# Two linked model blocks on one core: the up projections of the MLPs as 64-row matmuls in pairs

## The chip, the cores and the metric

One core of a Trainium2 chip runs the whole program in one launch. The metric is device microseconds (us) of that core. The kernel before was run twice: 2519.97 and 2526.85 us, median 2523.41 us.

## The reference

Two blocks of a language model work one after the other on one sequence of 512 tokens with width 1024, in float32. The first holds a gated convolution branch, a recurrent branch and an MLP; the second holds an HGRN mixer with an MLP and an attention layer with low-rank keys and values with another MLP. Only the MLPs bear on this case. There are three, all of the same form:

```
h = rms_norm(x, g)                              # 512 x 1024
f = square(relu(h @ w_up))                      # 512 x 4096
x = x + f @ w_down                              # 512 x 1024
```

## The kernel before

All activations lie feature-major: a tile is 128 features (partitions) x 512 tokens, X has KD = 8 of them, and a matmul contracts over the 128 partitions of a weight tile and an activation tile and writes 128 x 512 sums into one of eight PSUM banks (`ps`). So that float32 accuracy comes out of matmuls on fp32r operands, every operand is split in two: a high part (XH, FH, w_hi), which is the value rounded to fp32r, and a low part (XL, FL, w_lo), which is what the rounding lost. A product is three matmuls, high x high, high weight x low activation, low weight x high activation (`product`, L1479 to L1486).

Weights come in chunks of 128 x 2048 values (1 MB), which hold two output tiles x eight contraction steps. There are two slots, 0 and 1, for raw, w_hi and w_lo, and chunk c uses slot c % 2. For each chunk SyncE loads `raw` (`load8`), ScalarE writes w_hi (`split_hi`, L549 to L553: it waits until TensorE has finished chunk c - 2, by the count of `halves`), GpSimd writes w_lo (`split_lo`, L529 to L533) and TensorE waits for that (`chunk_in`, L1500). TensorE counts up `halves` once per output tile, twice per chunk.

Each MLP (`mlp_pe`, L1605) has four quarters of the hidden width. A quarter is four up chunks (`up`, two per pass, j = 0 and 1, slots 0 and 1) and four down chunks (`down`). Up chunk j writes its two tiles to banks 2j and 2j + 1. In steady state `half8` computes the first tile entirely, 24 matmuls, and then the second (L1504). The first chunk of an MLP goes through `pair` (L1507) instead: step k of both tiles, then step k + 1, each waiting for tile k of XL, because its input is still being made; the matmul for the squares' sum of the norm (`squares_pe`) follows it. The down chunks do the same with FH and FL as input (`pair` for j = 0, `half8` for j = 1).

Behind TensorE, VectorE takes each up tile in turn (`mlp_dve`, L1146): it waits for `halves`, scales and clamps the bank into `tmp` (L1157), squares (L1160) and subtracts the high part that ScalarE writes (L707) to get FL (L1163). ScalarE, behind its second tile of a chunk, splits the weights of the chunk two further on (`mlp_act`, L700):

```
for j in range(4):
    act.wait_ge(*at(n, "t", 8 * q + 4 * i + j + 5))
    act.activation(FH[...], tmp[:, j % 2:j % 2 + 1], ACT.Square)...
    if j % 2:
        split_hi(8 * q + 2 * i + c + j // 2 + 2, j // 2)
```

So the order of the work around the change is set by each engine's own program, written out by hand, and by counted semaphores between them. Just before each MLP, a residual sum brings the tiles of X one after the other; ScalarE makes XH (L336) and VectorE makes XL of it (L352), tile by tile.

Of the kernel before, what the change touches and what calls it, by code (L numbers as in the profile page):

```python
# [11 lines left out]
KD = D // P  # L12
# [54 lines left out]
def build_program(nc, a, out):  # L67
    ctx = ExitStack()
    with ctx:
        top = [nc.sbuf_base + (-nc.sbuf_base) % 32]  # L70

        def place(name, shape, dt, at=None):

            size = int(np.prod(shape[1:])) * (1 if dt == U8 else 4)
            where = top[0] if at is None else at
            if at is None:
                top[0] += size + (-size) % 32
            return nc.alloc_sbuf_tensor_at(name, list(shape), dt, offset=where), where

        def sem(name):  # L80
            return ctx.enter_context(nc.semaphore(name))
# [3 lines left out]
        w_hi, _ = place("w_hi", [P, 2, 2048], F32R)  # L85
        w_lo, _ = place("w_lo", [P, 2, 2048], F32R)
# [85 lines left out]
        ps = ctx.enter_context(nc.psum_tensor("ps", [P, 8, T], F32))  # L172
# [5 lines left out]
        halves = sem("halves")  # L178
# [10 lines left out]
        def s_(name):  # L189

            if name not in S_:
                S_[name] = sem(name)
            return S_[name]
# [25 lines left out]
        def signals(n, what):  # L219

            if kind_of[n] == "norm":
                if what in ("hi", "lo"):
                    return 0 if n == "n_fin1" else KD
                return 1 if what in ("ln", "inv") else KD
            if kind_of[n] == "scaled":
                if what in ("hi", "lo"):
                    return KD
                return 0 if n in ("n_hg", "n_mla") else {"sq": KD, "add": KD - 1, "mean": 1, "ln": 1, "inv": 1}[what]
            if kind_of[n] == "small":
                return 1 if what in ("mean", "ln", "inv") else 2  # L230
            return {"mlp": {"t": 4 + 32, "sq": 32, "fh": 32, "fl": 4 + 32, "dn": 4 + 32}, "sum": {"x": 4 + KD}}[kind_of[n]][what]

        def sig(n, what):

            return s_(kind_of[n] + "_" + what)

        def at(n, what, value):

            stages = kinds[kind_of[n]]
            return sig(n, what), value + sum(signals(m, what) for m in stages[:stages.index(n)])  # L240
# [11 lines left out]
        def w8(t, s, n):  # L252

            v = t[:, s].rearrange("p (k n) -> p k n", k=8)
            return [v[:, k, n * P:(n + 1) * P] for k in range(8)]
# [109 lines left out]
        def squares_pe(pe, n):  # L365

            pe.wait_ge(*at(n, "add", KD - 1))
            pe.matmul(ps[:, 7], ones[:], rst[:, 0], start=True, stop=True).then_inc(sig(n, "mean"), 1)
# [1099 lines left out]
        def _(pe):  # L1468
            pe.sem_inc(halves, 4)
            pe.wait_ge(ident_in, 16)  # L1470
            for k in range(KD):
# [3 lines left out]
                for b in range(TB):  # L1475
                    mm = pe.transpose(ps[:, k % 4, b * P:(b + 1) * P], x_tm[:, b, k * P:(k + 1) * P], ident[:])
                mm.then_inc(s_("x_turned"), 1)

            def product(dst, his, los, xh, xl, start=True, stop=True):  # L1479

                n = len(his)
                for k in range(n):
                    pe.matmul(dst, his[k], xh[k], start=start and k == 0, stop=False)  # L1483
                    pe.matmul(dst, his[k], xl[k], start=False, stop=False)  # L1484
                    mm = pe.matmul(dst, los[k], xh[k], start=False, stop=stop and k == n - 1)  # L1485
                return mm  # L1486
# [10 lines left out]
            def tiles(t, n=KD, first=0):  # L1497
                return [t[:, first + k] for k in range(n)]

            def chunk_in(c):  # L1500

                pe.wait_ge(lo_done, c + 3)

            def half8(s, n, bank, xh, xl):  # L1504
                product(ps[:, bank], w8(w_hi, s, n), w8(w_lo, s, n), tiles(xh), tiles(xl)).then_inc(halves, 1)

            def pair(s, bank, xh, xl, ready=None):  # L1507

                h = [w8(w_hi, s, n) for n in range(2)]
                l = [w8(w_lo, s, n) for n in range(2)]  # L1510
                for k in range(KD):
                    if ready is not None:
                        pe.wait_ge(*ready(k))
                    for n in range(2):
                        dst = ps[:, bank + n]
                        pe.matmul(dst, h[n][k], xh[:, k], start=k == 0, stop=False)  # L1516
                        pe.matmul(dst, h[n][k], xl[:, k], start=False, stop=False)  # L1517
                        mm = pe.matmul(dst, l[n][k], xh[:, k], start=False, stop=k == KD - 1)  # L1518
                        if k == KD - 1:
                            mm.then_inc(halves, 1)  # L1520
# [4 lines left out]
            def plain(c, iters, ev, xh, xl, ready=None):  # L1525

                with pe.Fori(0, iters) as i:
                    for j in range(2):
                        chunk_in(2 * i + c + j)
                        pe.wait_ge(*ev(4 * i + 2 * j + 2))  # L1530
                        if j == 0 and ready is not None:
                            pair(0, 0, xh, xl, ready)
                        else:
                            half8(j, 0, 2 * j, xh, xl)
                            half8(j, 1, 2 * j + 1, xh, xl)
# [11 lines left out]
            for k in range(KD):  # L1547
                mm = pe.matmul(ps[:, 7], ones[:], CO[:, k], start=k == 0, stop=k == KD - 1)
# [53 lines left out]
            single(FIRST["bo"], RT, lambda v: (s_("yb_evac"), v), VGH, VGL, BO_BANKS, lambda k: (s_("vg_lo"), k + 1))  # L1602
            plain(FIRST["wo"], 2, lambda v: at("wo", "x", v), MH, ML, lambda k: (s_("ml_done"), k + 1))

            def mlp_pe(n, xh, xl):  # L1605

                c = FIRST[n]

                def up(q, i, first=False):
                    for j in range(2):  # L1610
                        chunk_in(8 * q + 2 * i + c + j)
                        pe.wait_ge(*at(n, "dn", 8 * q + 2 * j + 2))
                        pe.wait_ge(*at(n, "t", 8 * q + 4 * i + 2 * j + 2))
                        if first and j == 0:
                            pair(0, 0, xh, xl, lambda k: at("n_" + n, "lo", k + 1))
                            squares_pe(pe, "n_" + n)
                        else:
                            half8(j, 0, 2 * j, xh, xl)
                            half8(j, 1, 2 * j + 1, xh, xl)

                def down(q):
                    with pe.Fori(0, 2) as i:
                        for j in range(2):
                            chunk_in(8 * q + 2 * i + c + 4 + j)
                            if j:
                                pe.wait_ge(*at(n, "t", 8 * q + 12))
                            pe.wait_ge(*at(n, "dn", 8 * q + 4 * i + 2 * j + 2))
                            if j == 0:
                                pe.wait_ge(*at(n, "t", 8 * q + 10))

                                pair(0, 0, FH, FL, lambda k: at(n, "fl", 8 * q + 5 + k))
                            else:
                                half8(1, 0, 2, FH, FL)
                                half8(1, 1, 3, FH, FL)

                up(0, 0, first=True)
                up(0, 1)
                down(0)
                with pe.Fori(1, 4) as q:
                    with pe.Fori(0, 2) as i:  # L1640
                        up(q, i)
                    down(q)
# [124 lines left out]
            with pe.Fori(0, 4) as i:  # L1767
                def part(t, s, at, k, step, n):
                    return [t[:, s, at + q * step:at + q * step + n] for q in range(k)]
# [4 lines left out]
                for h in range(4):  # L1774
                    mm = product(ps[:, h], part(w_hi, 0, h * P, 2, 512, P), part(w_lo, 0, h * P, 2, 512, P),
                                 tiles(CQH, 2), tiles(CQL, 2))
                mm.then_inc(halves, 1)
                for h in range(2):
                    mm = product(ps[:, 4 + h], part(w_hi, 0, 1024 + h * P, 2, 256, P),
                                 part(w_lo, 0, 1024 + h * P, 2, 256, P), tiles(CQH, 2), tiles(CQL, 2))  # L1780
# [3 lines left out]
                for h in range(4):  # L1784
                    if h == 0:
                        pe.wait_ge(*at("ckv", "lo", 2))
                    pe.wait_ge(*att("qn_done", 4 * i + h + 1))
                    mm = product(ps[:, h], part(w_hi, 1, h * P, 2, 512, P), part(w_lo, 1, h * P, 2, 512, P),
                                 tiles(CKH, 2), tiles(CKL, 2))
# [7 lines left out]
                for b in range(TB):  # L1797
                    if b == 2:
                        pe.wait_ge(*att("qr_done", 2 * i + 2))
                    mm = product_x(ps[:, 4 + b], part(w_hi, 1, 1024, 2, 512, 512), part(w_lo, 1, 1024, 2, 512, 512),  # L1800
                                   [CKH[:, k, b * P:(b + 1) * P] for k in range(2)],
                                   [CKL[:, k, b * P:(b + 1) * P] for k in range(2)])
# [57 lines left out]
            for b in range(TB):  # L1860
                mm = pe.matmul(ps[:, 7, b:b + 1], rst[:, 0, b * P:(b + 1) * P], ones[:, 0:1], start=True, stop=True)
# [74 lines left out]
```

## Time and profile before

| | |
|---|---|
| median of two runs | 2523.41 us (2519.97 to 2526.85) |
| the profiled execution, its own time | 2520.08 us |
| its span, first to last instruction | 2518.3 us |
| mean granted TensorE clock | 0.967 |
| TensorE busy | 2343.5 us, 93% of the span, 10216 matmuls |
| TensorE's weight loads | 1847.8 us, beside the matmuls |
| VectorE, ScalarE, GpSimd busy | 1256.6, 910.9 and 864.5 us |

Two records stand for each matmul: its weight load (PEld) and the matmul (PE). A matmul's row runs from where it starts to where its results are written, and the next one starts before that end, so the number that counts for throughput is the distance between two starts, the pitch. In a group's name `128*128` stands for the rows and columns of weights and `128x512` for the moving operand; `64*128` is a matmul of 64 rows. The granted clock is given as a share of 2.4 GHz; 0.50 is 1.2 GHz.

### The profile page before, as it was taken

Reading aid. Unit: us, or ns where it says so; the run is one execution under the profiler, and the core shown is the slowest. Engines: PE = TensorE matmul, PEld = TensorE weight load, DVE = VectorE, ACT = ScalarE, POOL = GpSimd, SP = SyncE. Lnnn points to the kernel's source line nnn. Section 1 sums busy time; section 2 is a strip of 40 time slices with the busy share of each in tenths; the row PEclk is TensorE's granted clock in tenths of the full one; section 3 lists DMA queues with packets and bytes.
Section 4 is the critical chain, followed back from the end, with each engine's and each line's share of the span. In section 5 each row is a group of like instructions: output and inputs, shape, how many; then the busy total and the mean of one; then the engine's idle time right before and its main releaser. Section 6 shows DMA issues by size and latency. Waiting matters only on the chain.

```text
span 2518.3 us, 29967 instructions
## 1 busy us (share of the span) xinstructions
PE 2343.5 (93%) x10216; PEld 1847.8 (73%) x10216; DVE 1256.6 (50%) x1917; ACT 910.9 (36%) x1127; POOL 864.5 (34%) x189
## 2 busy tenths in 40 slices
PE   7999988699999998899979999997888889999998
PEld 5888767477788886778857888885566568788886
DVE  4999377625332237887756233245544521522333
ACT  5423366423221226466543222225444422322223
POOL 2344333253434433222213444344111104344442
PEclk9999989799999999899989999999999999999999
DMA  3322311132232232221102232322111103223322
GB/s 123 100 94 90 100 43 43 50 99 94 85 99 90 93 100 78 56 65 52 61 24 97 97 100 84 100 83 79 34 29 33 33 17 89 95 84 100 99 84 100
DMA packets 232935, 193.85 MB, mean 77 GB/s; under 512 B 18224, under 2 KB 228656, under 8 KB 232880
## 3 DMA queue, kind: packets, MB, share of 16 engines
q1 hardware_dynamic: 232016, 191.92, 24.4%
q10 hardware_dynamic: 864, 1.21, 0.2%
q8 instruction: 32, 0.52, 0.1%
q14 instruction: 23, 0.19, 0.0%
HBM read 191.01 MB, written 2.10 MB: 77 GB/s over the span
## 4 chain that ended last, share of the span: by engine, by line
issue 60%; PE 24%; POOL 13%; DVE 1%; ACT 1%; POOLq 0%; DMA 0%; DVEq 0%; SPq 0%; ACTq 0%
POOL w_lo L532 13%; PE ps L1483 6%; PE ps L1485 6%; PE ps L1484 6%; PE ps L1516 2%; PE ps L1518 2%; PE ps L1517 2%; ACT w_hi L553 0%; DMA x_tm<-in_x 0%; POOLq L542 0%; DVE CO L1032 0%; DVE tmp L323 0%; DVE ps L1017 0%; PE ps L312 0%; DVE ps L1021 0%
## 5 line engine op out<-in xcount | busy, mean ns | idle before, releaser
L532 POOL TENSOR_TENSOR w_lo<-raw,w_hi 128x2048 fp32r<-128x2048 f32 x184 | 862.5, 4688 | 1623.9 <-ACT w_hi L553 1623.9
L553 ACT ACTIVATE w_hi<-raw 128x2048 fp32r<-128x2048 f32 x184 | 351.2, 1909 | 542.8 <-PE ps L1485 300.2
L1483 PE MATMUL ps<-XH,w_hi 128*128 128x512 f32 x1128 | 450.4, 399 | 12.6 <-POOL w_lo L532 9.5
L1485 PE MATMUL ps<-XH,w_lo 128*128 128x512 f32 x1128 | 447.4, 397 | 0.0
L1484 PE MATMUL ps<-XL,w_hi 128*128 128x512 f32 x1128 | 447.4, 397 | 0.0
L1483 PEld LDWEIGHTS ps<-XH,w_hi 128*128 128x128 f32 x1128 | 212.6, 188 | 68.4 <-POOL w_lo L532 11.6
L1484 PEld LDWEIGHTS ps<-XL,w_hi 128*128 128x128 f32 x1128 | 212.5, 188 | 52.7 <-issue 1.4
L1485 PEld LDWEIGHTS ps<-XH,w_lo 128*128 128x128 f32 x1128 | 212.5, 188 | 52.3
L1171 DVE TENSOR_TENSOR X<-X,ps 128x512 f32 x72 | 49.5, 688 | 339.2 <-PE ps L1485 176.8
L707 ACT ACTIVATE FH<-tmp 128x512 f32 x96 | 60.7, 632 | 382.9 <-DVE tmp L1157 382.9
L1157 DVE SCALAR_TENSOR_TENSOR tmp<-ps,rst 128x512 f32<-128x512 f32 x96 | 66.3, 690 | 257.0 <-PE ps L1485 242.5
L1516 PE MATMUL ps<-XH,w_hi 128*128 128x512 f32 x448 | 182.2, 407 | 12.2 <-DVE XL L328 10.2
L1517 PE MATMUL ps<-XL,w_hi 128*128 128x512 f32 x448 | 178.4, 398 | 0.0
L1518 PE MATMUL ps<-XH,w_lo 128*128 128x512 f32 x448 | 178.1, 398 | 0.0
L1516 PE MATMUL ps<-FH,w_hi 128*128 128x512 f32 x384 | 151.7, 395 | 0.0
L1517 PE MATMUL ps<-FL,w_hi 128*128 128x512 f32 x384 | 151.7, 395 | 0.0
L1518 PE MATMUL ps<-FH,w_lo 128*128 128x512 f32 x384 | 151.7, 395 | 0.0
L1483 PE MATMUL ps<-FH,w_hi 128*128 128x512 f32 x384 | 151.7, 395 | 0.0
L1484 PE MATMUL ps<-FL,w_hi 128*128 128x512 f32 x384 | 151.7, 395 | 0.0
L1485 PE MATMUL ps<-FH,w_lo 128*128 128x512 f32 x384 | 151.7, 395 | 0.0
L979 DVE SCALAR_TENSOR_TENSOR ps<-UP,vec,ps 128x512 f32<-128x512 f32 x224 | 148.2, 747 | 0.0
L1160 DVE TENSOR_TENSOR tmp<-tmp 128x512 f32<-128x512 f32 x96 | 113.5, 1182 | 3.3
(326 smaller groups left out, 3660.9 us busy)
## 6 DMA issues: line engine op xcount, KB each, us to landing
raw<-in_mlp_w_down SPq DMA_DIRECT2D x68, 512.0 KB, 4.1
raw<-in_w SPq DMA_DIRECT2D x64, 512.0 KB, 4.4
raw<-in_mlp_w_up SPq DMA_DIRECT2D x64, 512.0 KB, 4.2
raw<-in_w_in SPq DMA_DIRECT2D x56, 512.0 KB, 4.4
raw<-in_mla_w_o SPq DMA_DIRECT2D x16, 512.0 KB, 4.6
raw<-in_w_b_out SPq DMA_DIRECT2D x16, 384.0 KB, 4.0
raw<-in_w_a_out SPq DMA_DIRECT2D x8, 512.0 KB, 3.9
raw<-in_w_o SPq DMA_DIRECT2D x8, 512.0 KB, 4.0
```

The source lines that it names most:

```text
L532: pool.tensor_tensor(w_lo[:, s], raw[:, s], w_hi[:, s].bitcast(F32), ALU.subtract)\
L553: act.activation(w_hi[:, s], raw[:, s], ACT.Copy).then_inc(hi_done, 1)
L707: act.activation(FH[:, bass.ds(4 * i + j, 1)], tmp[:, j % 2:j % 2 + 1], ACT.Square)\
L979: dve.scalar_tensor_tensor(dst, src, w, acc, ALU.mult, ALU.add).then_inc(cs, 1)
L1157: dve.scalar_tensor_tensor(t, ps[:, j:j + 1], 0.0, rst[:, 1:2], ALU.max, ALU.mult)\
L1160: dve.tensor_tensor(t2, t, t, ALU.mult).then_inc(sig(n, "sq"), 1)
L1483: pe.matmul(dst, his[k], xh[k], start=start and k == 0, stop=False)
L1484: pe.matmul(dst, his[k], xl[k], start=False, stop=False)
L1485: mm = pe.matmul(dst, los[k], xh[k], start=False, stop=stop and k == n - 1)
L1516: pe.matmul(dst, h[n][k], xh[:, k], start=k == 0, stop=False)
L1517: pe.matmul(dst, h[n][k], xl[:, k], start=False, stop=False)
L1518: mm = pe.matmul(dst, l[n][k], xh[:, k], start=False, stop=k == KD - 1)
```

## The change

A function `pair_rows` takes the place of `pair` and of the two `half8` in the up chunks of all three MLPs. It cuts each contraction step of 128 rows into two of 64. In a first turn tile n = 0 gets its products over rows 0 to 63 of all eight steps and tile n = 1 those over rows 64 to 127, alternating matmul by matmul; in a second turn the row halves are exchanged. The two tiles have banks of their own, so no bank is written by both halves at once; between the turns TensorE waits on a new semaphore `rows_turn`, which the last matmul of either tile in the first turn counts up. `halves` is counted up twice at the end of the second turn. The waits for XL of the first chunk stand in the first turn. The down chunks and all else stay as they are, on the other engines too.

```diff
--- before.py
+++ after.py
@@ -1602,6 +1602,24 @@
             single(FIRST["bo"], RT, lambda v: (s_("yb_evac"), v), VGH, VGL, BO_BANKS, lambda k: (s_("vg_lo"), k + 1))
             plain(FIRST["wo"], 2, lambda v: at("wo", "x", v), MH, ML, lambda k: (s_("ml_done"), k + 1))
 
+            def pair_rows(s, bank, xh, xl, turned, ready=None):
+
+                h = [w8(w_hi, s, n) for n in range(2)]
+                l = [w8(w_lo, s, n) for n in range(2)]
+                for turn in range(2):
+                    if turn:
+                        pe.wait_ge(s_("rows_turn"), turned)
+                    for k in range(KD):
+                        if ready is not None and turn == 0:
+                            pe.wait_ge(*ready(k))
+                        for p, (w, x) in enumerate(((h, xh), (h, xl), (l, xh))):
+                            for n in range(2):
+                                r = slice(64 * (n ^ turn), 64 * (n ^ turn) + 64)
+                                mm = pe.matmul(ps[:, bank + n], w[n][k][r], x[r, k],
+                                               start=turn == 0 and k == 0 and p == 0, stop=turn == 1 and k == KD - 1 and p == 2)
+                                if k == KD - 1 and p == 2:
+                                    mm.then_inc(halves if turn else s_("rows_turn"), 1)
+
             def mlp_pe(n, xh, xl):
 
                 c = FIRST[n]
@@ -1612,11 +1630,12 @@
                         pe.wait_ge(*at(n, "dn", 8 * q + 2 * j + 2))
                         pe.wait_ge(*at(n, "t", 8 * q + 4 * i + 2 * j + 2))
                         if first and j == 0:
-                            pair(0, 0, xh, xl, lambda k: at("n_" + n, "lo", k + 1))
+                            turned = 32 * ("mlp0", "mlp1", "mlp2").index(n) + 8 * q + 4 * i + 2 * j + 2
+                            pair_rows(0, 0, xh, xl, turned, lambda k: at("n_" + n, "lo", k + 1))
                             squares_pe(pe, "n_" + n)
                         else:
-                            half8(j, 0, 2 * j, xh, xl)
-                            half8(j, 1, 2 * j + 1, xh, xl)
+                            turned = 32 * ("mlp0", "mlp1", "mlp2").index(n) + 8 * q + 4 * i + 2 * j + 2
+                            pair_rows(j, 2 * j, xh, xl, turned)
 
                 def down(q):
                     with pe.Fori(0, 2) as i:
```

On TensorE, the first up chunk of an MLP before the change (rows of one program; ps is PSUM, `scaled_lo` counts the tiles of XL), from its first wait on:

```order
L1516 MATMUL ps<-XH,w_hi 128x512 [waits mlp_t,scaled_lo,mlp_dn,lo_done]
L1517 MATMUL ps<-XL,w_hi 128x512
L1518 MATMUL ps<-XH,w_lo 128x512
L1516 MATMUL ps<-XH,w_hi 128x512
L1517 MATMUL ps<-XL,w_hi 128x512
L1518 MATMUL ps<-XH,w_lo 128x512
L1516 MATMUL ps<-XH,w_hi 128x512 [waits scaled_lo]
```

And the same place after the change:

```order
L1618 MATMUL ps<-XH,w_hi 128x512 [waits mlp_t,scaled_lo,mlp_dn,lo_done]
L1618 MATMUL ps<-XH,w_hi 128x512
L1618 MATMUL ps<-XL,w_hi 128x512 x2
L1618 MATMUL ps<-XH,w_lo 128x512 x2
L1618 MATMUL ps<-XH,w_hi 128x512 [waits scaled_lo]
```

Each step between two waits still has six matmuls, but each has 64 rows where it had 128 (the rows give the columns alone), so the waits for XL stand half as much work apart.

On TensorE further on in the same chunk after the change, where the first turn ends and the second begins (no such wait was there before):

```order
L1618 MATMUL ps<-XH,w_hi 128x512 [waits scaled_lo]
L1618 MATMUL ps<-XH,w_hi 128x512
L1618 MATMUL ps<-XL,w_hi 128x512 x2
L1618 MATMUL ps<-XH,w_lo 128x512 x2
L1618 MATMUL ps<-XH,w_hi 128x512 [waits rows_turn]
L1618 MATMUL ps<-XH,w_hi 128x512
```

The wait on `rows_turn` is new, and the second turn's 48 matmuls stand behind it; every up chunk has it, 48 times in all.

## Rows read from the trace of the kernel before

**Rows 1.** The page: TensorE's and the others' totals, and the two weight splits.
```profile
PE 2343.5 (93%) x10216; PEld 1847.8 (73%) x10216; DVE 1256.6 (50%) x1917; ACT 910.9 (36%) x1127; POOL 864.5 (34%) x189
...
L532 POOL TENSOR_TENSOR w_lo<-raw,w_hi 128x2048 fp32r<-128x2048 f32 x184 | 862.5, 4688 | 1623.9 <-ACT w_hi L553 1623.9
L553 ACT ACTIVATE w_hi<-raw 128x2048 fp32r<-128x2048 f32 x184 | 351.2, 1909 | 542.8 <-PE ps L1485 300.2
```

**Rows 2.** Busy us by stretch, granted clock behind POOL's; ScalarE's timeline: start, us.
```profile
850.00:950.00 100.00, 100.00 (x430) 80.34 (x429) 33.61 (x37) 25.37 (x23) 41.51 (x9) 1.00 0.30 95
...
852.22 1.92 ACT L553 ACTIVATE w_hi<-raw 128x2048 fp32r<-128x2048 f32 x1 [7.93 <-PE ps L1518]
863.42 1.92 ACT L553 ACTIVATE w_hi<-raw 128x2048 fp32r<-128x2048 f32 x1 [9.28 <-PE ps L1485]
```

**Rows 3.** Timeline, start and us: matmuls and weight loads in steady state.
```profile
642.02 0.39 PE L1483 MATMUL ps<-XH,w_hi 128*128 128x512 f32 x1
642.26 0.40 PE L1484 MATMUL ps<-XL,w_hi 128*128 128x512 f32 x1
...
642.26 0.19 PEld L1485 LDWEIGHTS ps<-XH,w_lo 128*128 128x128 f32 x1
642.49 0.19 PEld L1483 LDWEIGHTS ps<-XH,w_hi 128*128 128x128 f32 x1
```

**Rows 4.** Timeline after a wait of the third up chunk; granted clock by stretch.
```profile
632.74 4.78 POOL L532 TENSOR_TENSOR w_lo<-raw,w_hi 128x2048 fp32r<-128x2048 f32 x1 [14.55 <-ACT w_hi L553]
637.57 0.19 PEld L1483 LDWEIGHTS ps<-XH,w_hi 128*128 128x128 f32 x1 [3.27 <-POOL w_lo L532]
637.57 0.50 PE L1483 MATMUL ps<-XH,w_hi 128*128 128x512 f32 x1 [2.83 <-POOL w_lo L532]
637.68 0.19 PEld L1484 LDWEIGHTS ps<-XL,w_hi 128*128 128x128 f32 x1
...
637.90 0.55 PE L1484 MATMUL ps<-XL,w_hi 128*128 128x512 f32 x1
...
639.54 0.63 PE L1485 MATMUL ps<-XH,w_lo 128*128 128x512 f32 x1
...
639.96 0.63 PE L1483 MATMUL ps<-XH,w_hi 128*128 128x512 f32 x1
...
638.00:641.00 3.00, 3.00 (x9) 2.32 (x8) 2.05 (x4) 2.20 (x2) 0.00 (x0) 0.50 0.67 216
```

**Rows 5.** Timeline: plain f32 matmuls of 64 and 128 rows, and short matmuls.
```profile
1808.42 0.91 PE L1812 MATMUL ps<-KR,QR 64*128 64x384 f32 x2
1809.26 1.13 PE L1811 MATMUL ps<-KN,QN 128*128 128x512 f32 x2
1810.31 1.12 PE L1812 MATMUL ps<-KR,QR 64*128 64x512 f32 x2
...
1068.16 3.09 PE L1680 MATMUL ps<-HE 128*128 128x64 f32 x25
```

**Rows 6.** Timelines of VectorE and ScalarE behind the first MLP's first up chunk.
```profile
627.10 0.69 DVE L1157 SCALAR_TENSOR_TENSOR tmp<-ps,rst 128x512 f32<-128x512 f32 x1 [0.61 <-DVE small L1197]
...
629.39 0.68 DVE L1157 SCALAR_TENSOR_TENSOR tmp<-ps,rst 128x512 f32<-128x512 f32 x1
...
630.22 0.63 ACT L707 ACTIVATE FH<-tmp 128x512 f32 x1 [1.67 <-DVE tmp L1157]
630.76 1.90 ACT L553 ACTIVATE w_hi<-raw 128x2048 fp32r<-128x2048 f32 x1
```

**Rows 7.** Timelines: start of the second and third MLPs' first chunks, XL's last tiles.
```profile
1348.58 0.40 PE L1516 MATMUL ps<-XH,w_hi 128*128 128x512 f32 x1
...
1351.40 4.60 DVE L352 SCALAR_TENSOR_TENSOR XL<-X,vec,XH 128x512 fp32r<-128x512 f32 x1 [1.93 <-ACT XH L336]
...
1356.53 0.74 DVE L352 SCALAR_TENSOR_TENSOR XL<-X,vec,XH 128x512 fp32r<-128x512 f32 x1
...
2142.06 0.39 PE L1516 MATMUL ps<-XH,w_hi 128*128 128x512 f32 x1
...
2144.88 4.60 DVE L352 SCALAR_TENSOR_TENSOR XL<-X,vec,XH 128x512 fp32r<-128x512 f32 x1 [0.67 <-ACT XH L336]
```

## The prediction

> **What bounds the kernel now.** I read the page's totals first. TensorE is busy 93% of the span, and the two slowest helpers, GpSimd's low half of the weights and ScalarE's high half, stay far below it [rows 1]. Next I took the busy times by stretch: in the middle of an MLP TensorE is busy 100.00 of 100 us with 430 matmuls at the full granted clock [rows 2]. So inside the MLPs the matmuls themselves are the bound, and the other engines matter only where they come late. The pitch of a matmul (start to start) comes from the distance of two weight splits, one per chunk of 48 matmuls: 863.42 - 852.22 = 11.20 us, or 0.2333 us each [rows 2]. In the order of time each weight load starts together with the matmul before its own and lies beside it [rows 3]. A row of 0.39 to 0.40 us is the way from start to written result, longer than the pitch, since matmuls are pipelined.
>
> What fills the 0.233 us? Just after 3 us without work the granted clock is 0.50, 1.2 of 2.4 GHz, and the pitch there is 639.96 - 639.54 = 0.42 to 0.43 us [rows 4], so streaming 512 columns costs 0.427 there and 0.213 at 2.4 GHz. That leaves 0.020 us per matmul which only the full clock shows. After an idle engine two loads start 0.11 us apart and the second matmul starts 0.33 us after the first, 0.10 more than the pitch [rows 4]: a load occupies about 0.107 us, and it is paid for only where nothing streams beside it.
>
> **The change, part by part.** Each up chunk had 2 tiles x 8 steps x 3 products = 48 matmuls of 128 rows. It now has 96 of 64 rows, as 48 pairs: one half on rows 0 to 63 into one bank, the other on rows 64 to 127 into the other. 3 MLPs x 16 chunks x 48 = 2304 pairs stand for 2304 matmuls.
>
> *The pairs.* The trace has no two matmuls side by side, so the pair's pitch must be bounded. From below: both halves stream 512 columns, 0.213 us, and a pair needs two loads of 0.107 us, again 0.214; in a stretch of short matmuls 25 loads with their matmuls take 3.09 us, 0.12 each, or 0.24 for two [rows 5]. So a pair can hardly beat 0.214, and the loads could hold it at 0.24. From above: nothing lies side by side, and each half costs a full pitch, 0.467; a 64-row matmul alone is no shorter than a 128-row one (1.12 against 1.13 us for two [rows 5]). The value nearest to a row is the present pitch, 0.233: the same columns, the same bytes per partition, and loads that fill but don't exceed it. So the pairs cost 0 us; their bounds are (0.214 - 0.233) x 2304 = -44 us and +0.233 x 2304 = +537 us.
>
> The Trainium skill knows such pairs. Its page "TensorE: Matmul & The Clock Gate", section "Part 3: Packing small matmuls — row/col tiling", has matmuls in different row groups run at once, a pack lasting one matmul plus some 4 ns per further tile. By that a pair would be 0.237 us and the pairs +9 us, an estimate from that page; no run here shows it yet.
>
> *The turn.* Between the two halves of a chunk TensorE waits on its own last matmuls (`rows_turn`). The last start is followed by 0.395 us until its result is written [rows 3], about 0.05 us until a waiting TensorE goes on (GpSimd ends at 632.74 + 4.78 = 637.52, TensorE starts at 637.57 [rows 4]) and a load with nothing beside it, 0.107: 0.55 us, less the 0.12 (half a pair's pitch) after which the next half would have come anyway, is 0.44 us. 48 turns would be 21 us. Three of them, in the second chunk of each MLP, lie inside the 2.6 to 2.8 us that TensorE waits for weights anyway [rows 4]; the three of the first chunks I count below. 42 x 0.44 = 18.5 us. All other instructions of the engine stand behind that wait, but its queue is only matmuls of the same chunk, so nobody else waits on it. Bounds: 0.1 us each if the drain is partly hidden (4 us), 0.8 us (34 us).
>
> *The first chunk of each MLP.* It begins before its input is complete: step k waits for the low half XL of tile k. It took 1.40 us per step; the first turn now takes 0.70 and runs into the tiles that come last. In the second MLP the chunk starts at 1348.58; the seventh XL, stretched to 4.60 us beside GpSimd, is there at 1356.00 and the eighth at 1357.27 [rows 7]. The turn would want the seventh at 1348.58 + 6 x 0.70 = 1352.78, so it waits 3.2 us and ends at 1357.97; then 0.44 and 8 x 0.70 = 5.6 us give 1364.0, against 1348.58 + 11.20 = 1359.8 before: +4.2 us. For the first MLP, fed by a sum of the same kind, I take the same +4.2. In the third the eighth XL is there at 2144.88 + 4.60 = 2149.48, wanted at 2142.06 + 4.9 [rows 7]: ends at 2156.2 against 2153.3, +3.0. What follows hangs on the end of this chunk (the squares' sum, the scale, the first outputs), so it is all paid: 11.4 us. A fallen clock after 3 us of idling, as at 637.57 [rows 4], may add up to 1.6 us each time, 0 to 5 us; I take none.
>
> *Both outputs at once.* Before, the first tile of a chunk was ready 5.6 us before the second; now both come at its end, and VectorE takes them one behind the other before ScalarE may split the weights two chunks on. This order is on record: after the first chunk of an MLP both tiles already wait. VectorE's first row starts at 627.10, its second tile at 629.39, ScalarE's output row at 630.22, its split at 630.76 [rows 6], GpSimd's at 632.74, and TensorE goes on at 637.57 [rows 4]: 10.5 us from the end of a chunk. The chunk in between lasts 11.2 + 0.44 us, less 0.16 by which a start comes before the previous result. So some 1.0 us is left, and 0.5 where a down chunk without a turn stands between. It costs 0, but the cover is thin: every 1 us that this chain gets longer beyond that costs 1 us per chunk, 48 us in all. The down products get their last FL tile 2.3 us later than before (629.39 - 627.10 [rows 6]), but want it only in the last of eight steps, 7 x 1.4 = 9.8 us in.
>
> *Sum.* 0 + 18.5 + 11.4 = 29.9 us on the profiled execution's 2520.08 us gives 2550.0. The median of the runs is 3.3 us above that execution, so I forecast 2553 us, 1.2% slower, which counts as no change: about 2% is what a measurement of this kernel can tell.
>
> **The rivals.**
> *The halves don't run side by side (slower).* If a matmul of the upper rows waits until that of the lower rows is through, a pair costs 0.467 us: +537 us, and with turns (the first chunks then feed in time) +20: about 3080 us. For it: no two matmuls overlap by more than their pipeline in this trace, and the operands are of the type that the split rows call fp32r [rows 1], of which no 64-row matmul is in the trace. Against it: nothing in the work forces it, since the halves share neither rows nor banks. It decides as soon as a pair is above 0.245 us, where the total passes 2%.
>
> *A load doesn't hide within its row half (slower).* In the plain f32 form it is not hidden: the 64x384 rows take 1809.26 - 1808.42 = 0.84 us for two and the 128x512 rows 1.05, so 128 columns cost 0.105 and the 512 columns 0.42, with 0.105 over, a load [rows 5]. With each half as 0.213 + 0.107 = 0.320 per pair the change costs 0.087 x 2304 = 200 us: about 2753 us. Against it: rows 3 hide the load in exactly our form. The Trainium skill, on the same page "TensorE: Matmul & The Clock Gate", section "Part 3: Packing small matmuls — row/col tiling", says that loads overlap a running matmul only where the row groups differ; rows 3 contradict that at 128 rows (a load of the same rows beside the matmul at a pitch of 0.233), and a pair that obeyed it would be this rival.
>
> *Each load takes a little of the stream (slower).* If the 0.020 us are the load's price, a pair with two loads is 0.253: +46 us, 2599 us.
>
> *The overhead vanishes (no change, or faster).* If the 0.020 us are the price of exchanging weights under a stream, and the other half covers it, a pair is at the loads' 0.218: -35 us, 2518 us. To be over 2% faster it would need more than the whole 0.020 us and free turns, which streaming excludes.
>
> **How the numbers follow.** Forecast 0.54 (a tenth of it above 2574 us), vanishing overhead 0.07 (0.02 of it past 2%), load takes stream 0.10, load not hidden 0.11, no overlap 0.18. Faster by over 2%: 0.02; within: 0.49 + 0.05 = 0.54; slower: 0.05 + 0.10 + 0.11 + 0.18 = 0.44. The range goes from 2500 (pairs at 0.214 and cheap turns) to 2790, over the unhidden load; it leaves out the serial case. The forecast's own range is 2510 to 2590.
>
> **What would show it.** In the timeline of the changed kernel's up chunks: two halves starting 0.1 us apart or together, and 0.233 us per pair (a chunk of 11.6 us between weight splits); 0.47 would be the serial case, 0.32 the unhidden load. One gap of about 0.4 us in the middle of each chunk; a wait of 3 us on VectorE's XL in the first chunk of the MLPs at the places above; TensorE's wait for GpSimd's w_lo not above the 2.6 to 2.8 us three times. Waits for w_lo in every chunk would say that the thin cover is gone, and the forecast wrong by tens of microseconds.

## The result, and the profile after

| | before | changed |
|---|---|---|
| median | 2523.41 us | 2558.15 us (2553.84 to 2562.47, two runs) |
| ratio | | 1.0134, 95% interval 1.01 to 1.0168 |
| profiled execution | 2520.08 us | 2553.84 us |
| span | 2518.3 us | 2552.1 us |
| the three MLPs together | 1089.7 us | 1122.2 us |
| the rest, up to the last matmul | 1420.9 us | 1422.2 us |

The last two rows are worked out from the starts of matmuls in the trace: an MLP goes from the first matmul of its first up chunk to the first one after its last down chunk. So 32.5 of the execution's 33.8 us arose in the MLPs. The forecast was 2553 us, and 29.9 us more in the MLPs.

The page of the changed kernel, totals and the two splits, which answer to [rows 1], and the new matmuls:

```profile
PE 2370.0 (93%) x12520; PEld 1849.7 (72%) x12520; DVE 1201.3 (47%) x1917; ACT 911.0 (36%) x1127; POOL 861.7 (34%) x189
...
L532 POOL TENSOR_TENSOR w_lo<-raw,w_hi 128x2048 fp32r<-128x2048 f32 x184 | 859.6, 4672 | 1660.5 <-ACT w_hi L553 1660.5
...
L1618 PE MATMUL ps<-XH,w_hi 64*128 64x512 f32 x1536 | 314.2, 404 | 18.1 <-DVE XL L352 8.2
L1618 PE MATMUL ps<-XL,w_hi 64*128 64x512 f32 x1536 | 306.8, 395 | 0.0
```

There are 12520 - 10216 = 2304 more matmuls, as counted, and TensorE is busy only 26.5 us longer. One row still lasts 0.395 us, yet 1536 of them are busy for 307 us, 0.2 each. They must lie side by side. Of the 18.1 us that the group stood idle, the page puts 8.2 down to VectorE's XL. That wait is new, and so are those of the 48 turns, which stand at the weight loads: on the page, 25.6 us of the loads' idle time are put down to TensorE's own matmuls of L1618.

TensorE's timeline in the middle of a chunk (start, us; `x2` merges the two halves of a pair) and its weight loads, which answer to [rows 3]:

```profile
728.50 0.40 PE L1618 MATMUL ps<-XH,w_hi 64*128 64x512 f32 x2
728.74 0.39 PE L1618 MATMUL ps<-XL,w_hi 64*128 64x512 f32 x2
728.97 0.40 PE L1618 MATMUL ps<-XH,w_lo 64*128 64x512 f32 x2
729.46 0.50 PE L1618 MATMUL ps<-XH,w_hi 64*128 64x512 f32 x2
729.80 0.39 PE L1618 MATMUL ps<-XL,w_hi 64*128 64x512 f32 x2
...
728.74 0.19 PEld L1618 LDWEIGHTS ps<-XH,w_lo 64*128 64x128 f32 x2
729.46 0.19 PEld L1618 LDWEIGHTS ps<-XH,w_hi 64*128 64x128 f32 x2 [0.53 <-PE ps L1618]
```

At full precision the halves of these pairs start 0.003 us apart, and so do their two loads (0.003 or 0.004 us in 1940 of the 2304 pairs, at most 0.019). The pairs start 0.233 us apart, and a merged row is no longer than that of one matmul. At 728.97 the turn comes: the next pair starts after 0.49 us and the one behind it after 0.34, since the load of the first pair after the turn has nothing to hide beside (its row is 0.50 long). That is 0.83 us for two distances that otherwise take 0.47, so a turn costs 0.36 us here; the steady chunks show 0.35 each.

The end of an up stage and the start of the next one, a place of which the prediction did not speak:

```profile
666.65 0.39 PE L1618 MATMUL ps<-XH,w_lo 64*128 64x512 f32 x2
666.98 0.50 PE L1516 MATMUL ps<-FH,w_hi 128*128 128x512 f32 x1
667.31 0.39 PE L1517 MATMUL ps<-FL,w_hi 128*128 128x512 f32 x1
667.54 0.40 PE L1518 MATMUL ps<-FH,w_lo 128*128 128x512 f32 x1
...
711.64 0.40 PE L1485 MATMUL ps<-FH,w_lo 128*128 128x512 f32 x1
711.97 0.50 PE L1618 MATMUL ps<-XH,w_hi 64*128 64x512 f32 x2
712.30 0.40 PE L1618 MATMUL ps<-XL,w_hi 64*128 64x512 f32 x2
```

From 64-row to 128-row matmuls the distances are 0.33 and 0.33 us in place of 0.233 twice, and back again the same: 0.19 us per crossing, and 21 such crossings between up and down stages. Again the first row behind it is 0.50 us long, as after a wait, though the view names no wait there.

The first chunk of the second MLP, TensorE and VectorE, which answer to [rows 7]:

```profile
1370.86 0.40 PE L1618 MATMUL ps<-XH,w_lo 64*128 64x512 f32 x2
1374.11 0.50 PE L1618 MATMUL ps<-XH,w_hi 64*128 64x512 f32 x2 [2.85 <-DVE XL L352]
...
1369.51 4.54 DVE L352 SCALAR_TENSOR_TENSOR XL<-X,vec,XH 128x512 fp32r<-128x512 f32 x1 [1.93 <-ACT XH L336]
```

The seventh XL ends at 1369.51 + 4.54 = 1374.05 and TensorE goes on at 1374.11, 3.25 us after the pair before. Less the 0.23 us of a pair, that is 3.0 us of waiting, where the forecast had 3.2.

The cover behind a steady chunk, VectorE, ScalarE and GpSimd after the chunk that ends at 906.56, and TensorE's first matmul on the weights (917.95):

```profile
906.69 0.69 DVE L1157 SCALAR_TENSOR_TENSOR tmp<-ps,rst 128x512 f32<-128x512 f32 x1 [11.03 <-PE ps L1618]
...
908.97 0.68 DVE L1157 SCALAR_TENSOR_TENSOR tmp<-ps,rst 128x512 f32<-128x512 f32 x1
...
910.33 1.90 ACT L553 ACTIVATE w_hi<-raw 128x2048 fp32r<-128x2048 f32 x1
...
912.31 4.62 POOL L532 TENSOR_TENSOR w_lo<-raw,w_hi 128x2048 fp32r<-128x2048 f32 x1 [10.84 <-ACT w_hi L553]
...
917.95 0.40 PE L1618 MATMUL ps<-XH,w_hi 64*128 64x512 f32 x2
```

Both tiles wait at the end, the second 2.28 us behind the first, and the weights are ready at 912.31 + 4.62 = 916.93, 10.4 us after the chunk's end and 1.0 us before they are wanted.

The third chunk of each MLP differs from the steady ones by the clock, and not by the change. With the granted clock at 0.50 for a stretch at its start, behind the wait for w_lo, it is some 1.5 us longer. Before, that came about in the first and second MLP (chunks of 12.85, 12.84 and 11.31 us), after the change in the first and third (13.20, 11.67 and 13.19 us). The last column but two is the granted clock, at the start of the third chunk of the first and of the second MLP after the change:

```profile
642.00:645.00 3.00, 2.87 (x14) 2.30 (x16) 2.61 (x4) 0.77 (x2) 0.08 (x1) 0.57 0.49 138
1397.00:1400.00 3.00, 3.00 (x26) 2.44 (x28) 2.51 (x5) 0.94 (x2) 0.00 (x0) 1.00 0.58 173
```

Two of three fell in either trace, so the comparison of the two is not disturbed by it; the experiments below differ in how many fell.

### The profile page after: what moved, and what is told of

The parts are those of the page before. It is cut to its first block, busy times and chain, and to the rows that moved or that the text cites. A ratio compares the mean times of both kernels' runs of the same rounds, so it can differ in the third digit from the quotient of the medians.

```text
span 2552.1 us, 34599 instructions
## 1 busy us (share of the span) xinstructions
PE 2370.0 (93%) x12520; PEld 1849.7 (72%) x12520; DVE 1201.3 (47%) x1917; ACT 911.0 (36%) x1127; POOL 861.7 (34%) x189
## 4 chain that ended last, share of the span: by engine, by line
issue 61%; PE 24%; POOL 12%; DVE 1%; ACT 1%; POOLq 0%; DMA 0%; DVEq 0%; SPq 0%; ACTq 0%
POOL w_lo L532 12%; PE ps L1618 6%; PE ps L1483 4%; PE ps L1484 4%; PE ps L1485 4%; PE ps L1516 2%; PE ps L1517 2%; PE ps L1518 2%; ACT w_hi L553 0%; DMA x_tm<-in_x 0%; POOLq L542 0%; DVE CO L1032 0%; PE ps L1476 0%; DVE tmp L323 0%; DVE ps L1017 0%
## 5 line engine op out<-in xcount | busy, mean ns | idle before, releaser
L1618 PE MATMUL ps<-XH,w_hi 64*128 64x512 f32 x1536 | 314.2, 404 | 18.1 <-DVE XL L352 8.2
L1618 PE MATMUL ps<-XL,w_hi 64*128 64x512 f32 x1536 | 306.8, 395 | 0.0
L1618 PE MATMUL ps<-XH,w_lo 64*128 64x512 f32 x1536 | 306.7, 394 | 0.0
L1618 PEld LDWEIGHTS ps<-XH,w_hi 64*128 64x128 f32 x1536 | 146.1, 186 | 81.5 <-PE ps L1618 25.6
L1516 PE MATMUL ps<-XH,w_hi 128*128 128x512 f32 x400 | 163.8, 409 | 10.4 <-DVE XL L328 10.2
L1618 PEld LDWEIGHTS ps<-XH,w_lo 64*128 64x128 f32 x1536 | 146.3, 186 | 34.7
L1618 PEld LDWEIGHTS ps<-XL,w_hi 64*128 64x128 f32 x1536 | 146.4, 186 | 31.3
L1483 PE MATMUL ps<-XH,w_hi 128*128 128x512 f32 x408 | 163.2, 400 | 4.8 <-DVE XL L352 3.4
L1484 PE MATMUL ps<-XL,w_hi 128*128 128x512 f32 x408 | 161.9, 397 | 0.0
L1485 PE MATMUL ps<-XH,w_lo 128*128 128x512 f32 x408 | 161.8, 397 | 0.0
L1517 PE MATMUL ps<-XL,w_hi 128*128 128x512 f32 x400 | 159.9, 400 | 0.0
L1518 PE MATMUL ps<-XH,w_lo 128*128 128x512 f32 x400 | 159.5, 399 | 0.0
L1484 PE MATMUL ps<-FL,w_hi 128*128 128x512 f32 x384 | 151.7, 395 | 0.0
```

The lines of the kernel that those rows point to most:

```text
L1618: mm = pe.matmul(ps[:, bank + n], w[n][k][r], x[r, k], start=turn == 0 and k == 0 and p == 0, stop=turn == 1 and k == KD - 1 and p == 2)
```

## The experiments

The theory after this reading: the pairs cost nothing, and the 32.5 us are turns, first chunks and crossings. Each experiment names its rival. Chunk lengths below are distances from a chunk's first matmul to that of the next chunk (for the first chunk of an MLP, to the squares' matmul behind it); the time of the three MLPs is compared because the rest, which no kernel here changes, alone took from 1420.5 to 1430.9 us in the profiled executions.

**No exchange: what is a turn?**

```diff
-                    if turn:
-                        pe.wait_ge(s_("rows_turn"), turned)
...
-                                r = slice(64 * (n ^ turn), 64 * (n ^ turn) + 64)
+                                r = slice(64 * n, 64 * n + 64)
...
```

> The changed kernel without its turn: in the second turn each tile takes the same row half again (tile 0 rows 0 to 63, tile 1 rows 64 to 127), so nothing has to wait and the wait on rows_turn goes. It computes the products over half of the rows twice and leaves the other half out; count, shapes and loads of all matmuls are those of the changed kernel. Theory (the turn is a drain of TensorE, 0.35 us by the changed kernel's trace: two distances of 0.485 and 0.335 us where 2 x 0.233 is the rule): no distance over 0.24 us inside a chunk, chunks of 11.2 us in place of 11.55, and 45 to 48 x 0.35 = 16 to 17 us less than the changed kernel, 2541 us. Rival (the turn costs because weights of the other row half must be brought in, wait or not): the same as the changed kernel's 2558 us.

Measured: 2543.75 us, against 2526.51 for before on that chip, ratio 1.0066 (1.0049 to 1.0083). The steady chunks are 11.20 us, those before and behind a down stage 11.29 with half a crossing in them, and the MLPs take 1108.4 us, 13.8 less than in the changed kernel. (42 steady chunks x 0.35 are 14.7. The first chunks together grew by 0.9, since that of the second MLP now met a granted clock of 0.50 behind its wait.) The first chunks keep 16.64, 16.50 and 15.39 us: without a turn, but with their wait for XL. This run takes out the wait and the exchange together, so by itself it can't tell which of the two costs. The changed kernel can. Between two up chunks the tiles change row halves too, into other banks and without a wait, and the pairs there stand 0.23 us apart, as everywhere (the chunk that begins at 735.16):

```profile
734.93 0.40 PE L1618 MATMUL ps<-XH,w_lo 64*128 64x512 f32 x2
735.16 0.40 PE L1618 MATMUL ps<-XH,w_hi 64*128 64x512 f32 x2
735.39 0.39 PE L1618 MATMUL ps<-XL,w_hi 64*128 64x512 f32 x2
```

Both together show that the turn costs by its wait. The other row half's weights come for nothing.

**Both tiles on the same rows: what lets two matmuls run at once?**

```diff
-                                r = slice(64 * (n ^ turn), 64 * (n ^ turn) + 64)
+                                r = slice(64 * turn, 64 * turn + 64)
```

> The changed kernel with both tiles on the same row half at a time: rows 0 to 63 of both in the first turn, rows 64 to 127 of both in the second. Everything else, the output included, is as in the changed kernel. Theory (two 64-row matmuls run at once because they stand in different row halves of the array): each matmul now costs a full pitch, a pair 0.467 us, a chunk 22.4 us + 0.35, about 2304 x 0.233 = 537 us more: 3080 to 3095 us. Rival (they overlap because they write to different banks, or because a half-height matmul streams in half the time): about 2558 us.

Measured: 3038.58 us, one run. The timeline inside a turn:

```profile
680.41 0.62 PE L1618 MATMUL ps<-XH,w_lo 64*128 64x512 f32 x2
680.88 0.63 PE L1618 MATMUL ps<-XH,w_hi 64*128 64x512 f32 x2
681.35 0.62 PE L1618 MATMUL ps<-XL,w_hi 64*128 64x512 f32 x2
```

Two matmuls to two banks now stand 0.233 us apart and a merged row is 0.62 us long, in place of 0.40. The MLPs take 1608.6 us, 519 more than before. So it is the row half, not the bank and not the smaller height, that lets a pair run side by side. It came out 41 to 56 us under the expectation. Some 14 us of that is that the first chunks no longer wait for XL. Most of the rest is a remnant of the overlap: where an up chunk follows another, the last matmuls of the old one, on rows 64 to 127, lie beside the first of the new one, on rows 0 to 63, and from 902.94 to 903.51 the starts are 0.11 to 0.12 us apart (chunks of 21.9 to 22.4 us, expected 22.75).

**Four matmuls of 32 rows: do loads queue up?**

```diff
...
-                            for n in range(2):
-                                r = slice(64 * (n ^ turn), 64 * (n ^ turn) + 64)
-                                mm = pe.matmul(ps[:, bank + n], w[n][k][r], x[r, k],
+                            for n in range(4):
+                                r = slice(32 * n, 32 * n + 32)
+                                mm = pe.matmul(ps[:, bank + n if n < 2 else 2 + n], w[n % 2][k][r], x[r, k],
...
```

> The changed kernel with four matmuls of 32 rows in place of each pair of 64: rows 0 to 31, 32 to 63, 64 to 95, 96 to 127 into four banks (the two of the chunk and banks 4 and 5, which nothing reads), no exchange and no turn wait. What goes to banks 4 and 5 is left out of the output, and each kept part is added twice. Theory A (each row group has its own load and its own stream; what costs 0.020 us over the streaming is paid once per matmul inside a row group): four in 0.233 us, chunks of 11.2 us, 2541 us as without the turn. Theory B, the one of my forecast (weight loads go one after the other, 0.107 us each): four loads take 0.43 us, chunks of 20.5 us, 0.195 x 2304 = 450 us more, about 2990 us.

Measured: 2546.73 us, one run; matmuls and loads:

```profile
728.06 0.40 PE L1616 MATMUL ps<-XL,w_hi 32*128 32x512 f32 x4
728.29 0.40 PE L1616 MATMUL ps<-XH,w_lo 32*128 32x512 f32 x4
...
728.06 0.19 PEld L1616 LDWEIGHTS ps<-XH,w_lo 32*128 32x128 f32 x4
728.29 0.20 PEld L1616 LDWEIGHTS ps<-XH,w_hi 32*128 32x128 f32 x4
```

Four matmuls and four loads in 0.233 us, in chunks of 11.20 us: theory A. Up to four row groups load and stream beside one another. The 0.107 us of a load is no floor for a pair, and the pitch of 0.233 us, with its 0.020 us above the streaming time, is the same with one, two or four groups at work.

**The first chunk as before: what did it cost?**

```diff
-                            pair_rows(0, 0, xh, xl, turned, lambda k: at("n_" + n, "lo", k + 1))
+                            pair(0, 0, xh, xl, lambda k: at("n_" + n, "lo", k + 1))
+                            pe.sem_inc(s_("rows_turn"), 2)
```

> The changed kernel with the first up chunk of each MLP done as before the change (128 rows, each step of both tiles waiting for its XL), the other 45 in row halves. Theory (those chunks lose because their first turn asks for each XL after 0.70 in place of 1.40 us and then waits): they are back at 11.2 us from 16.5, 15.5 and 15.6, so 5.3 + 4.2 + 4.4 = 14 us less, 2544 us; TensorE's wait for w_lo before the third chunk stays near 2 to 3 us. Rival (the loss of these chunks is hidden behind that wait for w_lo): 2558 us.

Measured: 2542.57 us, ratio 1.0059 (1.0042 to 1.0075). The first chunks are back at 11.20 us, the MLPs at 1106.3 us, 15.9 less than in the changed kernel. The first chunks are 14.0 of it; another 1.6 came by the clock, since only one third chunk in place of two met the granted clock of 0.50. The wait for w_lo before the third chunk is still there, 1.88 us in the second MLP:

```profile
1386.53 0.49 PE L1618 MATMUL ps<-XH,w_hi 64*128 64x512 f32 x2 [1.88 <-POOL w_lo L532]
```

That wait hides the second chunk's turn, but nothing of the first chunk's, as forecast.

**A single 64-row matmul in the kernel before: is the crossing a cost of its own?** In 90 tiles the matmul of step 4, high x high, takes 64 rows:

```diff
+                        r = slice(0, 64) if k == 4 and p == 0 else slice(0, P)
+                        mm = pe.matmul(ps[:, bank], w[k][r], x[r, k], start=k == 0 and p == 0,
...
```

> The kernel before, in which one matmul of each up tile that half8 computed (step 4, high x high, 90 tiles in all) has 64 rows in place of 128; the products of rows 64 to 127 of that step are left out. Theory (TensorE pays for going between the 128-row and the 64-row form: in the changed kernel 0.19 us at either crossing, seen as a first distance of 0.32 to 0.33 and a second of 0.33 where 0.233 is the rule): three distances of 0.33 in place of 0.233 per tile, 0.3 to 0.38 us x 90 = 26 to 34 us more than before, 2550 to 2557 us. Rival (the 0.19 us belongs to two halves starting together, or to the change of the weights' tile): the same as before, 2523 us.

Measured: 2558.29 us, ratio 1.0121 (1.0104 to 1.0138) over 2525.94. The timeline:

```profile
734.93 0.40 PE L1611 MATMUL ps<-XH,w_lo 128*128 128x512 f32 x1
735.25 0.50 PE L1611 MATMUL ps<-XH,w_hi 64*128 64x512 f32 x1
735.69 0.50 PE L1611 MATMUL ps<-XL,w_hi 128*128 128x512 f32 x1
736.02 0.39 PE L1611 MATMUL ps<-XH,w_lo 128*128 128x512 f32 x1
```

Three distances of 0.32, 0.44 and 0.33 us in place of 0.70 in all, and chunks of 11.97 us in place of 11.20: 0.385 us per tile, two crossings of 0.19. The MLPs take 1120.7 us, 31.0 more than before (90 x 0.385 are 34.7; in the three second chunks the wait for w_lo hides 2.3 of it, and one third chunk fewer met the low clock). The crossing costs by itself, with no pair and no wait in sight. The Trainium skill says so: its page "TensorEngine Tiling (Array Packing)", section "Key Properties", has it that changing the tiling mode, not just the tile, drains the engine. The traces agree in that nothing of the new form starts beside the stream of the old one, and give the size, 0.19 us each way. It is less than a turn's 0.35, since the new load starts 0.32 to 0.33 us after the last matmul, 0.07 before that one's result is written, where the turn waits until it is written and 0.09 more. The row 0.50 long holds that load, 0.107 us with nothing to hide beside. What fills the other 0.08 to 0.09 us of a crossing no run here takes apart.

**More work for VectorE: how thin is the cover?** Each up tile's square is done three times, in the changed kernel and in the one before:

```diff
...
+                            for again in range(2):
+                                dve.tensor_tensor(t2, t, t, ALU.mult).then_inc(s_("sq_more"), 1)
+                                dve.wait_ge(s_("sq_more"), more + again + 1)
```

> The changed kernel with VectorE's square of every up tile done three times in place of once (same result), which makes the way from a chunk's end to the weights two chunks on 1.45 us longer (two more rows of 0.69 us between the first tile's square and the second tile's first row). Theory (both outputs at once leave a thin cover: 10.35 us from chunk end to ready weights, against 11.4 us until they are wanted behind an up chunk and 11.1 behind a down chunk): the cover is gone by 0.3 to 0.7 us, TensorE waits for w_lo two or three times per quarter, about 1 us per quarter and 12 us in all, 2570 us. Rival (more room than that): the same as the changed kernel, 2558 us.

> The kernel before with the same two more squares per up tile. Theory (before the change the first tile is out of the way 5.6 us before the chunk ends, and from the chunk's end to ready weights it is 8.0 us with no square on the way): the same as before, 2523 us, with at most 1 to 5 us in the first chunks of the MLPs, where both tiles wait together. Rival (the way of the second tile is crowded too, since the first tile's squares collide with GpSimd's row): 10 us or more above before.

Measured: the changed kernel goes to 2587.53 us, ratio 1.0228 (1.0203 to 1.0253), 29 us above the changed kernel's median; its MLPs take 1151.8 us, 29.6 more. The kernel before goes to 2537.14 us, 1.0043 (1.0025 to 1.0061); its MLPs take 1097.1 us, 7.4 more, all of it in the second and third chunks; its steady chunks stay at 11.20. 4.0 us of that are the second chunks, behind which TensorE waits for weights whose way starts with both tiles waiting together. 3.4 are the third chunks, of which all three now met a granted clock of 0.50, two of them for twice as long as before. In the changed kernel every other steady up chunk grows from 11.6 to 12.5 us. One of them:

```profile
914.17 0.69 DVE L1157 SCALAR_TENSOR_TENSOR tmp<-ps,rst 128x512 f32<-128x512 f32 x1 [11.04 <-PE ps L1622]
...
917.81 0.68 DVE L1157 SCALAR_TENSOR_TENSOR tmp<-ps,rst 128x512 f32<-128x512 f32 x1
...
919.17 1.91 ACT L553 ACTIVATE w_hi<-raw 128x2048 fp32r<-128x2048 f32 x1
...
921.15 4.85 POOL L532 TENSOR_TENSOR w_lo<-raw,w_hi 128x2048 fp32r<-128x2048 f32 x1 [12.23 <-ACT w_hi L553]
...
926.28 0.50 PE L1622 MATMUL ps<-XH,w_hi 64*128 64x512 f32 x2 [0.70 <-POOL w_lo L532]
```

The second tile comes 3.64 us behind the first (2.28 without the extra squares), GpSimd's row is 4.85 us (4.62), and the weights are taken up 12.25 us after the chunk's end at 914.03 where 11.4 was the time for it. So the cover of 1.0 us is real and thin. My price for going beyond it was less than half of what it cost: I had added only VectorE's own rows, not the longer row of GpSimd, nor that 0.28 us lie between its end and TensorE's start where 0.05 did in [rows 4]. The trace shows what stands there: TensorE has passed the wait for w_lo at 926.04, 0.04 us after GpSimd's end, and then works through what follows it in the loop for two more waits (L1634 and L1635, recorded at 926.04 and 926.14) before its load starts at 926.27.

**No exchange and the first chunk as before: do the parts add up?** Both edits together.

> The changed kernel without its turn (second turn on the same row halves again, as in the run without the exchange: half of the rows counted twice, the other half left out) and with the first up chunk of each MLP as before. What is left of the change is the pairs themselves in 45 chunks and the crossings between 64-row and 128-row matmuls, 24 of them at 0.19 us. Theory (the parts add up: pairs 0, turns, first chunks, crossings): the three MLPs together take 4 to 5 us more than the 1089.7 us of before in the traces, and the median lies 3 to 8 us above the kernel before, 2527 to 2534 us, hardly to be told from it. Rival (a pair is a little slower than a full matmul wherever they run, hidden so far in the other terms): 15 us or more above before.

Measured: 2529.14 us over 12 runs against 2527.14 over 17, ratio 1.0014 (1.0002 to 1.0025). The MLPs take 1091.5 us, 1.9 more than before: 24 crossings at 0.19 are 4.6. Three of them, behind the squares' matmuls, are hidden by the wait for w_lo, and 0.7 us more is given back there: the third chunk starts 14.82, 14.62 and 14.62 us after the squares' matmul where it started after 15.05, 14.85 and 14.83. Another 1.6 us is the clock, since one third chunk in place of two met the lower one. So 4.0 - 0.7 - 1.6 = 1.7 was to be expected. A pair costs what a matmul of full height costs, on the whole kernel as in the rows.

## Why the prediction was right, point by point

**Pairs at 0 us: right, in part for a wrong reason.** The pitch is 0.233 us. But I had counted two loads as 0.214 us one after the other and called them a second limit; they run side by side, and even four do. The Trainium skill's rule of some 4 ns per further tile ("TensorE: Matmul & The Clock Gate", section "Part 3: Packing small matmuls — row/col tiling") agrees with the trace, 0.003 us between the halves' starts, though the pitch of a pair does not grow by it. Of the rivals, no overlap (0.18), the unhidden load (0.11) and the load that takes stream (0.10) are all refuted for this form; the serial case is what the same-rows run shows. The overhead of 0.020 us did not vanish either. (One sum beside them was off: a pair of 0.245 us would have made 2580 us; the 2% are passed at 0.242.)

**The turn, 18.5 us: 14.7.** I had 0.44 us, measured is 0.35. The term that was off is "less the 0.12 (half a pair's pitch)". The halves don't start staggered but together, so a full 0.233 must be taken off, and the release took 0.09 us where I had 0.05. By the starts at full precision the last pair at 728.976 is written at 729.369 and the next load starts at 729.461: 0.393 + 0.092 + 0.107 - 0.233 = 0.36 us.

**The first chunks, 11.4 us: 14.0, the mechanism right.** Their lengths grew by 5.3, 4.2 and 4.4 us, where 4.2, 4.2 and 3.0 were forecast. The second MLP met the forecast to 0.1 us. In the others the granted clock fell after the wait, for 1.1 and 1.4 us more, a bound I had named and taken as nothing (granted clock in the last column but two):

```profile
619.00:622.00 3.00, 2.91 (x14) 1.68 (x14) 0.82 (x2) 0.00 (x0) 0.00 (x0) 0.51 0.98 324
...
1375.00:1378.00 3.00, 2.61 (x22) 1.78 (x22) 0.92 (x2) 0.00 (x0) 0.00 (x0) 1.00 0.96 311
2172.00:2175.00 3.00, 2.91 (x14) 2.13 (x14) 0.00 (x0) 0.00 (x0) 0.00 (x0) 0.50 0.97 317
```

The distances across the waits were 3.25, 3.25 and 2.57 us from start to start; the first and third were followed by 3 us at 1.2 GHz, the second was not, and why is not shown.

**The crossings, not in the sum: 4.0 us.** The prediction has no term for going from one height to the other. [rows 5], in which plain f32 matmuls of 64 and 128 rows alternate, couldn't show it: that form leaves its load uncovered anyway, and an uncovered load is more than half of what a crossing costs here.

**The second chunk, its turn hidden: right, and it hides more.** The squares' matmul behind each first chunk, of 128 rows among pairs, adds two crossings each, and the distance from it to the second chunk's first matmul grew from 0.46 to 1.06 us. Only part of that is real, since before the change the row behind the squares' matmul is recorded early and drawn out:

```profile
622.97 0.79 PE L1483 MATMUL ps<-XH,w_hi 128*128 128x512 f32 x1
```

It is 0.40 us longer than a steady row. The second chunks, measured from that start, became 0.7 us shorter each. What counts is the sum of the two: the third chunk starts 14.93, 14.72 and 14.73 us after the squares' matmul, where it started after 15.05, 14.85 and 14.83. So the wait for w_lo hides the turn of the second chunk and the crossing behind the squares' matmul too, and 0.4 us in all is given back.

**Both outputs at once, 0: right.** 10.4 us against the forecast 10.5, a cover of 1.0 us against 1.0.

Together: 14.7 (turns) + 14.0 (first chunks) + 4.0 (the 21 crossings between up and down stages) - 0.4 (from the squares' matmul to the third chunk) = 32.3, against 32.5 measured. The forecast had 29.9. Its errors are turns too dear by 3.8 us, first chunks too cheap by 2.6 and crossings left out for 4.0. They partly cancel, and that the median lies within 5 us owes something to that, and to luck: the two runs alone are 8.6 us apart.

## What to carry to other kernels

Matmuls in different row groups of TensorE run side by side, loads and all, at the pitch of one. That makes up for height that would otherwise be empty; where each matmul already fills all 128 rows it wins nothing, and the exchange of halves, crossings to the full height and outputs that come together must be paid for. Before a stage is made to step twice as fast through its input, look at how fast that input is made. And a tile that used to be finished halfway is cover for the engines behind: when it comes together with the next, measure what is left.

## What the runs showed of the hardware that was not expected

- Loads of different row groups start beside one another (in 1962 of 2304 pairs 0.003 or 0.004 us apart, at most 0.018), and four matmuls of 32 rows with their four loads take 0.233 us, no more than one of 128 rows. Between the 64-row pairs the 0.020 us above the streaming time stays.
- A single 64-row matmul among 128-row ones costs 0.385 us, more than a whole matmul's pitch, without any wait in the program. A crossing doesn't wait until the last result is written: the new load starts 0.07 us before.
- Parts of the kernel that no edit touches differed by up to 10 us between profiled executions (1420.5 to 1430.9 us). Differences of a few microseconds are better read from the lengths of steady chunks, which repeat to 0.01 us, than from medians. Where a chunk follows a wait of 2 to 3 us, look at the granted clock first: whether it fell there changed from kernel to kernel and made 1.1 to 1.5 us each time.
